# A ring of 14 raw and 8 high half-slots in place of 11 double slots for the expert weights

## The reference

```python
def moe_swiglu(x, w_router, b_router, we_gate, we_up, we_down):
    logits = (x @ w_router).astype(jnp.float32) + b_router.astype(jnp.float32)
    top_v, top_i = lax.top_k(logits, TOP_K)
    top_w = jax.nn.softmax(top_v, axis=-1)
    gates = jnp.sum(jax.nn.one_hot(top_i, N_EXPERTS, dtype=jnp.float32) * top_w[..., None], axis=-2)
    out = jnp.zeros(x.shape, jnp.float32)
    for e in range(N_EXPERTS):
        out = out + gates[..., e:e + 1] * swiglu(x, we_gate[e], we_up[e], we_down[e]).astype(jnp.float32)
```

## Time and profile before

| | |
|---|---|
| time, median of 3 runs | 839.19 us (838.34 to 840.11) |
| time of the profiled execution | 839.77 us |
| span in its profile | 837.9 us |
| TensorE busy | 807.6 us (96%) |
| VectorE busy | 556.5 us (66%) |
| ScalarE busy | 409.3 us (49%) |
| DMA, all queues | 201.04 MB, mean 240 GB/s |
| HBM read | 198.51 MB |

### The profile page before, as it was taken

The page is one execution under the profiler, slowest core; times in us unless marked ns, Lnnn a source line. Parts: engine busy times, 40 slices in busy tenths (PEclk is TensorE's granted clock), DMA queues, the critical chain, the costliest instruction groups (busy, mean ns, idle before and its releaser), DMA issues.

```text
span 837.9 us, 13798 instructions
## 1 busy us (share of the span) xinstructions
PE 807.6 (96%) x5076; PEld 630.1 (75%) x5076; DVE 556.5 (66%) x1038; ACT 409.3 (49%) x624; POOL 153.2 (18%) x164
## 2 busy tenths in 40 slices
PE   9999999999999999999999999999999988999985
PEld 7488779999999999668778887887866343865322
DVE  8999577466756556578883999799854042972105
ACT  7886455365333440485562696776651022650102
POOL 3811132222434421352231000000000000000003
PEclk9999999999999999999999899999999999999997
DMA  9603625645555521930500798988999999999992
GB/s 298 212 1 111 253 92 165 210 159 156 176 152 151 161 92 51 242 118 4 210 1 1 299 419 311 371 284 290 411 363 406 422 418 423 420 415 422 420 410 79
DMA packets 89555, 201.04 MB, mean 240 GB/s; under 512 B 24224, under 2 KB 48048, under 8 KB 89488
## 3 DMA queue, kind: packets, MB, share of 16 engines
q1 hardware_dynamic: 88560, 199.12, 64.7%
q10 hardware_dynamic: 576, 0.59, 0.2%
q0 software_dynamic: 352, 0.44, 0.2%
HBM read 198.51 MB, written 1.61 MB: 239 GB/s over the span
## 4 chain that ended last, share of the span: by engine, by line
PE 74%; DVE 10%; SPq 5%; DMA 4%; issue 2%; ACT 2%; POOL 1%; DVEq 0%; POOLq 0%; ACTq 0%
PE ps L1356 8%; PE ps L1355 8%; PE ps L1357 8%; PE ps L1718 7%; SPq L779 4%; PE ps L1449 4%; PE ps L1573 4%; PE ps L1365 4%; PE ps L1703 3%; PE ps L1702 3%; PE ps L1705 3%; DMA wraw_g<-in_moe_w_gate 3%; PE ps L1845 3%; PE ps L1846 2%; PE ps L1849 2%
## 5 line engine op out<-in xcount | busy, mean ns | idle before, releaser
L1355 PE MATMUL ps<-Md,split_u 128*128 128x288 f32 x296 | 87.3, 295 | 0.0
L1357 PE MATMUL ps<-Md,split_u 128*128 128x288 f32 x296 | 86.8, 293 | 0.0
L835 POOL TENSOR_TENSOR hb<-hb 128x288 f32<-128x288 f32 x9 | 7.7, 861 | 386.2 <-ACT hb L1325 361.0
L1902 DVE TENSOR_TENSOR xb<-xb,ps 128x288 f32<-128x288 f32 x80 | 33.5, 450 | 50.8 <-PE ps L1750 23.9
L996 ACT ACTIVATE split_u<-raw 128x1024 fp32r<-128x1024 f32 (+1 forms) x39 | 40.3, 1034 | 44.3 <-PE ps L1357 44.3
L1902 DVE TENSOR_TENSOR wrnd_g<-wraw_g,wrnd_g 128x1376 fp32r<-128x1376 f32 (+2 forms) x37 | 52.7, 1446 | 11.6 <-ACT wrnd_g L1002 11.3
L1902 DVE TENSOR_TENSOR wrnd_d<-wraw_d,wrnd_d 128x1376 fp32r<-128x1376 f32 (+2 forms) x25 | 35.2, 1437 | 35.3 <-ACT wrnd_d L1002 35.3
L1356 PE MATMUL ps<-hbr,split_u 128*128 128x288 f32 x192 | 57.1, 297 | 0.0
L1902 DVE TENSOR_TENSOR wrnd_u<-wraw_u,wrnd_u 128x1376 fp32r<-128x1376 f32 (+2 forms) x40 | 56.0, 1436 | 0.0
L1357 PEld LDWEIGHTS ps<-Md,split_u 128*128 128x128 f32 x296 | 55.6, 188 | 0.0
L1355 PEld LDWEIGHTS ps<-Md,split_u 128*128 128x128 f32 x296 | 55.5, 188 | 0.1
(11 more groups left out here) (487 smaller groups left out, 2175.1 us busy)
## 6 DMA issues: line engine op xcount, KB each, us to landing
wraw_g<-in_moe_w_gate SPq DMA_DIRECT2D x31, 688.0 KB, 10.1
wraw_u<-in_moe_w_up SPq DMA_DIRECT2D x29, 688.0 KB, 17.3
wraw_d<-in_moe_w_gate SPq DMA_DIRECT2D x22, 688.0 KB, 9.6
wraw_g<-in_moe_w_down SPq DMA_DIRECT2D x28, 512.0 KB, 15.1
wraw_u<-in_moe_w_down SPq DMA_DIRECT2D x28, 512.0 KB, 12.6
raw<-in_ffn_w_gate SPq DMA_DIRECT2D x21, 512.0 KB, 4.1
raw<-in_ffn_w_up SPq DMA_DIRECT2D x21, 512.0 KB, 4.6
raw<-in_ffn_w_down SPq DMA_DIRECT2D x21, 512.0 KB, 3.6
```

Source lines behind the costliest of these rows:

```text
L1355: pe.matmul(out, w_hi, x_hi, start=start, stop=False)
L1357: return pe.matmul(out, w_lo, x_hi, start=False, stop=stop)
L1902: return dve.tensor_tensor(o, a, b, op)
```

## The change

The 11 double slots of the loop are taken apart into 22 halves. A wide chunk takes one raw half out of a ring of 14 (used in blocks of 14 and 13, so that a turn of the loop has 54) and one high half out of a ring of 8 (blocks of 8 and 7). The raw half is held from the load to TensorE's use, the high half only from ScalarE's rounding to TensorE's use. So SyncE's load waits for the chunk 13 or 14 before it, and ScalarE's rounding has a new wait on `w_used`, for the chunk 8 (at times 7) before it. 13 chunks are asked for ahead of the loop, not 10. Behind the loop a plan (`tail_plan`) gives out all 26 halves by age: a load takes the half that has been free longest (two for a pair), a rounding takes the most lately freed one that is at least 8 steps old. Landings are counted on semaphores that go with the order of landings, not with the half. The sizes, the order of chunks, the source of each DMA, and every matmul, rounding and subtraction are the same.

```diff
 NSLOT = 11
 EXTRA = 2
-FIRST = NSLOT - 1
-JOIN = 17
-TAIL_ORDER = (11, 12, 6, 7, 8, 9, 10, 0, 1, 2, 3, 4, 5)
+RAW_BLOCKS = (14, 13, 14, 13)
+HIGH_BLOCKS = (8, 8, 8, 8, 8, 7, 7)
+NRING = max(RAW_BLOCKS)
+assert NRING + max(HIGH_BLOCKS) == 2 * NSLOT
+FIRST = 13
+HIGH_LEAD = 8
...
-def used_before(n, final=False):
-
-    t = n - LEAD
-    if not final or t < JOIN:
-        return n + 1 - (FIRST if t % (2 * PER) < FIRST else NSLOT)
-    for a in range(t - 1, -2 * PER - 1, -1):
-        if (slot_of(a + LEAD, True) if a >= 0 else a % (2 * PER) % NSLOT) == slot_of(n, True):
-            return max(a + LEAD + 1, 1)
-    return None
...
+def in_loop(table, n):
+
+
+    t = (n - LEAD) % (2 * PER)
+    back = next(d for d in range(1, 2 * PER + 1) if table[t - d] == table[t])
+    return table[t], n - back
+
+
+def tail_plan():
+
+
+
+    free = {}
+    for n in range(FIRST - 2 * PER, FIRST):
+        for table in (LOOP_RAW, LOOP_HIGH):
+            free[in_loop(table, n)[0]] = n
+    tokens = list(range(2 * NSLOT, 2 * NSLOT + 2 * EXTRA))
+    free.update((j, FIRST) for j in tokens)
...
+    for n in range(FIRST, TOTAL):
+        order = sorted((j for j in free if n < TOTAL - 6 or j not in END_HALVES), key=lambda j: (free[j], j))
+        raws = order[:1 + small_step(n)]
+        used, fresh = max(free[j] for j in raws), any(j in tokens for j in raws)
+        high, high_used = None, None
+        if not small_step(n):
+            high = max((j for j in order[1:] if j not in tokens and free[j] <= n - HIGH_LEAD), key=lambda j: free[j])
+            high_used = free[high]
+            free[high] = n
+        for j in raws:
+            free[j] = n
...
+def raw_used(n, final=False):
+
+
+    return max((TAIL[n][1] if final and n >= FIRST else in_loop(LOOP_RAW, n)[1]) + 1, 1)
+
+
+def high_used(n, final=False):
+
+    return max((TAIL[n][4] if final and n >= FIRST else in_loop(LOOP_HIGH, n)[1]) + 1, 1)
...
             def wait_slot(n, i, final):
 
-                used = used_before(n, final)
-                if used is None:
-                    sp.wait_ge(gather_mm, i * 4 + 8)
-                else:
-                    sp.wait_ge(w_used, upto(i, 2 * PER, used))
+                sp.wait_ge(w_used, upto(i, 2 * PER, raw_used(n, final)))
...
                 r, w = extent(step_of(n, final))
                 wait_chunk(act, n, i, final)
+                if n >= FIRST or in_loop(LOOP_HIGH, n)[1] >= 0:
+                    act.wait_ge(w_used, upto(i, 2 * PER, high_used(n, final)))
                 act.activation(halves(n, final)[0][0:r, 0:w], raw_half(n, final)[0:r, 0:w], ACT.Copy).then_inc(w_hi, 1)
```

More of the change, by code:

```diff
@@ L128 @@
 END_BANK = (3, 4, 5, 0, 1, 2, 6, 7)
-LOOP_BYTES = [16 * sum(t % NSLOT == j for t in range(2 * PER)) for j in range(NSLOT)]
-assert len(STEPS) == PER and 2 * PER % NSLOT == NSLOT - 1 and FIRST > LEAD
+assert len(STEPS) == PER and FIRST == LEAD + ACT_AHEAD and sum(RAW_BLOCKS) == sum(HIGH_BLOCKS) == 2 * PER
+LOOP_RAW = [j for b in RAW_BLOCKS for j in range(b)]
+LOOP_HIGH = [NRING + j for b in HIGH_BLOCKS for j in range(b)]
+LOOP_BYTES = [16 * LOOP_RAW.count(j) for j in range(NRING)]
 def by_pool(n):
@@ L186, in step_of @@
     return STEPS[(n - LEAD) % PER]
+def in_loop(table, n):
[9 more added lines that the diff above has]
+    free.update((j, FIRST) for j in tokens)
+    arrived = {j: max(n for n in range(FIRST - 2 * PER, FIRST) if in_loop(LOOP_RAW, n)[0] == j) for j in range(NRING)}
+    arrived.update((NRING + j, -2 * PER) for j in range(NRAW))
+    plan, sure = {}, -2 * PER
+    for n in range(FIRST, TOTAL):
[9 more added lines that the diff above has]
+            free[j] = n
+        tokens = [j for j in tokens if j not in raws]
+        sure = max(sure, used)
+        landed = min(arrived, key=lambda j: arrived[j])
+        assert arrived[landed] <= sure
+        arrived[landed] = n
+        plan[n] = raws, used, fresh, high, high_used, landed
+    return plan
 def bc(ap, n):
@@ L201, in rows, with raw_halves, high_half, landing @@
     return P if kk < FT - 1 else (P, LAST)[hf]
+END_HALVES = (4, NSLOT + 4)
+TAIL = tail_plan()
+def raw_halves(n, final=False):
+    return TAIL[n][0] if final and n >= FIRST else [in_loop(LOOP_RAW, n)[0]]
+def high_half(n, final=False):
+    return TAIL[n][3] if final and n >= FIRST else in_loop(LOOP_HIGH, n)[0]
+def raw_used(n, final=False):
+    return max((TAIL[n][1] if final and n >= FIRST else in_loop(LOOP_RAW, n)[1]) + 1, 1)
+def high_used(n, final=False):
+    return max((TAIL[n][4] if final and n >= FIRST else in_loop(LOOP_HIGH, n)[1]) + 1, 1)
+def landing(n, final=False):
+    return TAIL[n][5] if final and n >= FIRST else in_loop(LOOP_RAW, n)[0]
+def landed_bytes(n, final=False):
+    return sum(32 if final and small_step(a) else 16
+               for a in range(n + 1) if landing(a, final) == landing(n, final))
 def build(nc, x_d, consts_d, cols_d, misc_d, w_in_d, w_out_d, b_d, c_d, glu_d, ln_d, wst_d, wss_d,
@@ L368, in build, with half_at, raw_pair @@
         hg_h, hg_l = [[b[:, c:c + 1024].rearrange("p (k s) -> p k s", k=KT) for b in (hbr, hgb)] for c in (0, 1024)]
-        def slot_at(s, g, u, d, m):
-            return (g, s) if s < 4 else (u, s - 4) if s < 8 else (d, s - 8) if s < NSLOT else (m, s - NSLOT)
+        def half_at(j, g, u, d, m):
+            s, side = (j, 0) if j < NSLOT else (j - NSLOT, 1) if j < 2 * NSLOT else (j // 2, j % 2)
+            where, k = (g, s) if s < 4 else (u, s - 4) if s < 8 else (d, s - 8) if s < NSLOT else (m, s - NSLOT)
+            return where[:, k * SLOT + side * FF:k * SLOT + (side + 1) * FF]
+        def raw_pair(n, final=True):
+            return [half_at(j, wraw_g, wraw_u, wraw_d, wraw_m) for j in raw_halves(n, final)]
         def raw_half(n, final=False):
-            where, k = slot_at(slot_of(n, final), wraw_g, wraw_u, wraw_d, wraw_m)
-            return where[:, k * SLOT:k * SLOT + FF]
+            return raw_pair(n, final)[0]
         def halves(n, final=False):
[L381 to L387, removed]
+            return [half_at(j, wrnd_g, wrnd_u, wrnd_d, wrnd_m)
+                    for j in (high_half(n, final), raw_halves(n, final)[0])]
         def split_slot(n):
@@ L495, in build @@
         chunk_used = sem("chunk_used")
-        w_in_slot = [sem(f"w_in_slot{j}") for j in range(NSLOT + EXTRA)]
+        w_in_slot = [sem(f"w_in_slot{j}") for j in range(NRING)]
         w_hi = sem("w_hi")
@@ L771, in load_expert_chunk @@
                 sp.dma_start(raw_half(n, final)[:, 0:w],
-                             source(e, row, step_of(n, final))).then_inc(w_in_slot[slot_of(n, final)], 16)
+                             source(e, row, step_of(n, final))).then_inc(landing_of(n, final), 16)
             def load_small_chunks(experts, n, i):
```

23 lines of the change are left out of this document (11 added, 12 removed).

## The result

The change takes 832.86 us (median of 5 runs, 831.95 to 835.15) where before takes 839.19: a ratio of 0.993, 95% interval 0.9913 to 0.9946. That is 6.3 us less, of which the forecast had 5.3. The profiled execution took 834.43 us, with a span of 832.5.

The account below looks back on a forecast made before the run. TensorE was taken to pace the wide experts and the weight stream the rest from about 625 us. Only the restart counted: 839.19 - 5.3 = 833.9 us, own range 832.9 to 834.8, wider range 831.0 to 836.5.

Parts of the forecast that it names:

- What bounds the kernel: Whole kernel: TensorE paces the loop's wide experts, the weight stream from about 625 us, then a fixed 21 us tail.
- The start: Ahead of the loop: chunks 10 to 12 asked for without a wait are only queued earlier; nothing by itself.
- The ring of 14 and 13: Loop loads wait for step n - 13 or n - 14; the stream moves ahead, costed at nothing for TensorE.
- The restart, where it pays: Tail pairs 32 to 35: earlier thresholds restart the stream sooner; smallest gain 5.1 us, 5.5 by landings, 5.3 taken.
- pair 33: Tail load waiting for step 19: smallest of the four candidate gains, 5.1 us, so taken to set the gain.
- Does TensorE follow?: Between 660 and 709 us TensorE waits 6.1 us for weights, so all of the 5.3 us arrives.
- The rival by which the loop gains too: Loop, 511 to 590 us: TensorE's 2.4 idle us vanish too, gain 7.7 us, 831.5 us; chance 0.12.
- The high halves: ScalarE's copy also waits for step n - 8; 2.5 us of cover remain at chunk 55, cost nothing.
- the slower rival: Ring of 8 starves TensorE, 3 us in each of four wide experts: 6.7 us slower, 845.9 us; chance 0.06.
- Tail halves by age: Tail from pair 34: thresholds as before, up to five steps looser or one step later; nothing gained or lost.
- What would show it: Trace signs: rate dip mostly gone, waits near 676 and 708 shrunk, small gate steps near 624.7, last weights near 811.
- the dip is mostly gone: Sign at 612 to 636 us: the fall of the DMA rate to 358 GB/s would mostly vanish.

Follow-up runs that it names:

- the ask of ten: The changed kernel with chunks 10 to 12 held behind steps 0 to 2, so ten are asked for at first; 834.00 us, ratio 0.9936.
- HIGH_LEAD 6: The changed kernel with the minimum age in steps of a tail half taken for rounding set to 6, not 8; 832.16 and 830.80 us in two runs.
- the second profile: The changed kernel run once more, unchanged, for another profile; 832.78 us, ratio 0.9928.

## Why the prediction was right, point by point

**What bounds the kernel.** Right. From 640 us on the stream is full before and after (419 and 420 GB/s), though the prediction reads about 420 GB/s from slice 28 on, where the page has it steadily only from slice 32. An earlier last landing ended the program earlier: from it to the end of the span lie 15.8 to 16.1 us in nine of the thirteen profiles and 17.6 to 17.7 in the other four (last section). The 816.48 that the prediction calls the last weights is the landing of pair 109, where the chain of waits leaves the stream; pair 112 lands at 820.34. The Trainium skill's limit of 358 GB/s for HBM to SBUF ("DMA: Bandwidth & Descriptors", section "Where 436 GB/s comes from") does not hold here: 419 or 420 GB/s over 170 us, in all profiles. One core is at work in every run of this case; what it would get beside a second one, no run shows.

**The start.** Right: the ask of ten gives 834.00 us, the same as the change within the intervals.

**The ring of 14 and 13.** This is the step that failed. I costed it "at nothing for TensorE", which holds (76.61 us of 79 before, 76.58 and 76.61 after). That it moves the stream ahead is said too ("It pays later, as distance"), but this distance has no term, and the sum reads as if the thresholds behind it gave the gain alone. With the loop's loads held as before, only 2.6 us of gain are left (3.0 by the ratio). The ring wins the distance, 1.8 MB or 4.3 us up to 590 us, that the tail then keeps.

**The restart, where it pays.** The size was right and half of the reason. The candidates were taken at pairs 32 to 35 alone, with "up to pair 32 the stream then always has work" for the rest. The sum is a minimum over all places that can hold the stream, and the experiments show three more of them: the loop (2.9 to 3.7 us lost if held as before), the chunks 13 to 26 (3.7 to 3.8), and step 13 for the chunks 27 to 30, which I did not price. By the earlier trace rows the last gives (624.7 - 612.4) - (3 x 1.26 + 3.36) = 5.2 us, with 1.26 us between the landings of `down` chunks, just as much as pair 33's 5.1. It is the one that binds in the trace: chunk 27 goes out as soon as step 13 ends, the rate is low in 614 to 622 us, and HIGH_LEAD 6, which moves it, gains 2 us. In the six profiles whose loads have the change's thresholds in front of pair 31 (two of the change, two with pair 31 held, ten chunks asked for, six high halves) chunk 26 lands 8.9 to 10.7 us ahead of the end of step 18 and chunk 29 only 4.2 to 5.0: most of what one stream is ahead of another is gone behind step 13. Pair 33, the prediction's smallest, does not bind: it lands 3.35 and 3.34 us behind pair 32 in the two profiles of the change, one pair's time. That the forecast came out right with two candidates of equal size, one of them unseen, is in part luck. Pair 31's threshold was rightly seen as what held the stream before: given back alone it costs 3.7 to 4.7 us, and one step less about 1.5, as counted.

**The size.** 5.3 us were forecast, and the measured 832.86 lies at the lower edge of the prediction's own range. The last pair lands 3.85 us earlier in the first profile and 5.04 in the second; both began the expert stage 0.4 to 0.8 us later (first weights issued at 465.59 and 465.97, 465.16 before), and the first lost 1.6 us to the clock at 570 us. 5.04 + 0.8 = 5.8 and 3.85 + 0.4 + 1.6 = 5.9 us, beside 6.3 and 5.6 between the medians. The half microsecond beyond the forecast was not traced further; it is inside what runs differ by. The spans of the two profiled executions differ by 5.4 us for another reason: 3.85 from the last landing and 1.6 because before has the long end (last section) and the change has not. How often the long end comes in the unprofiled runs of either, the record does not tell.

**Does TensorE follow?** Right: 6.1 us of waits in 660 to 709 us became 1.0 and 1.8, and it followed by a further 2 us with HIGH_LEAD 6. The rival by which the loop gains too had no cause here: TensorE's idle time in 511 to 590 us is the same 2.4 us, a wait for VectorE's product of the hidden layer.

**The high halves.** Right, with cover to spare: even a wait for step n - 6 costs nothing measurable, so the slower rival falls.

**Tail halves by age.** For pairs 34 and later nothing was seen; that the looser thresholds of the chunks 13 to 26 matter stood nowhere in the prediction.

**What would show it.** Right: the waits near 676 and 708 us (shrunk), the last weights near 811 (pair 109 at 812.73 and 811.54), small gate step 18 at 625.60 in the second profile, 626.99 in the first. Wrong: "the dip is mostly gone" (377 to 387 GB/s, 358 before, 420 full) and, in part, "the rates up to 590 stay low" (319 and 330, 307 before).

## What to carry to other kernels

When a stream is held back at several places in turn, its gain is the smallest over all of them, from the point at which it could first run ahead: list every threshold from there, also the ones that look harmless, before taking the minimum. A deeper ring in a stage that another engine paces gives nothing in that stage, but it stores distance for the next one, if nothing on the way gives it back. After the change read where the stream is still below its full rate: here one constant more brought 2 us of stream.

## What the runs showed that I had not expected

**TensorE's clock falls at places that differ between executions of one kernel.** The stretch at half clock (1.2 GHz) near 570 us stood in five of the twelve profiles of the change and its variants (the change's first, and those of four experiments) and not in that of before. It costs TensorE 1.6 us of the loop. In both kinds the same idle time stands ahead of it, here in the first profile of the change,
```profile
569.71 0.50 PE L1913 MATMUL ps<-wrnd_d,Me 128*128 128x512 f32 x1 [1.76 <-DVE Me L1970]
570.04 0.48 PE L1914 MATMUL ps<-wrnd_g,Me 128*128 128x512 f32 x1
570.32 0.63 PE L1913 MATMUL ps<-wrnd_d,Me 128*128 128x512 f32 x1
```
and in its second:
```profile
569.86 0.49 PE L1913 MATMUL ps<-wrnd_d,Me 128*128 128x512 f32 x1 [1.77 <-DVE Me L1970]
570.20 0.39 PE L1914 MATMUL ps<-wrnd_g,Me 128*128 128x512 f32 x1
570.42 0.40 PE L1913 MATMUL ps<-wrnd_d,Me 128*128 128x512 f32 x1
```
so the idle time alone does not decide it; what does stays open. So it is with the end: from TensorE's last expert step to the end of the span lie 14.6 us in nine profiles and 16.3 in four (before and three of the experiments), where another stretch of 3.4 us at half clock stands in between. A difference of 1 to 2 us between two single profiles says nothing before the granted clocks are compared.

**A stream that runs nearly dry loses by chance.** SyncE issues nothing for 4.3 us between the chunks 66 and 67: it loads the numbers of the next experts there, six TENSOR_LOAD of 0.26 to 0.28 us with register work between them. Chunk 67 lands behind chunk 66 by 1.67 us (one chunk's time, nothing lost) in some profiles and by up to 4.55 in others, with the same order and spacing of issues. In the change's first profile the queue does run dry: in 589 to 590 us the DMA engines move 132 GB/s, where the profile with pair 31 behind step 18, with the same issues up to there, has 402. Why the same issues drain at different times stays open.
